# The down projection of a hybrid encoder layer, as eleven tile products or as seven half products of Strassen's scheme

## The reference, cut to what matters

```python
def conv_ffn(h, w_up, conv_w, conv_b, w_down):
    z = h @ w_up                     # 512 x 1024 @ 1024 x 5632
    S = z.shape[1]
    zp = jnp.pad(z, ((0, 0), (CONV_W - 1, 0), (0, 0)))
    zc = conv_b
    for j in range(CONV_W):          # 3 taps along the tokens
        zc = zc + zp[:, j:j + S] * conv_w[j]
    a, u = jnp.split(zc, 2, axis=-1)
    return (jax.nn.silu(a) * u) @ w_down      # 512 x 2816 @ 2816 x 1024
...
    return rms_norm(x, final_norm_g)
```

## Time and profile before

| | |
|---|---|
| median of 3 runs | 965.34 us (965.14 to 965.41) |
| span of the profiled execution | 963.6 us |
| PE, weight loads, DVE, ACT, POOL busy | 99%, 83%, 58%, 41%, 4% |
| share of the chain that ended last | PE 91%, DVE 4%, ACT 3%, issue 1% |
| granted TensorE clock, mean of the core | 0.999 |
| DMA | 93.80 MB, 97 GB/s; 31.4% of the 16 engines |
| matmuls and weight loads | 4782 each |

### The profile page before, as it was taken

How to read it: one execution, slowest core, us unless ns; L and a number is a source line. 1 busy time by engine, 2 the same in 40 slices (tenths; PEclk the granted TensorE clock), 3 DMA queues, 4 the chain that set the end, 5 groups by cost and what they waited for, 6 DMA issues and landing times.

```text
span 963.6 us, 12000 instructions
## 1 busy us (share of the span) xinstructions
PE 951.7 (99%) x4782; PEld 796.8 (83%) x4782; DVE 563.3 (58%) x646; ACT 390.9 (41%) x427; POOL 34.6 (4%) x27
## 2 busy tenths in 40 slices
PE   8999999999999999999999999999999999999997
PEld 6899889777888788888888878888888888888886
DVE  5877654554677564466545548776777677711123
ACT  6473223332664552333333446444434444311122
POOL 1000000200000000000021005000000000000000
PEclk9999999999999999999999999999999999999999
DMA  7414212122232523333223224343333432222212
GB/s 253 160 44 131 73 59 88 46 79 62 66 95 81 178 76 97 98 98 120 90 91 126 79 75 131 88 127 92 87 87 104 113 87 87 92 103 111 88 44 88
DMA packets 121570, 93.80 MB, mean 97 GB/s; under 512 B 3930, under 2 KB 115902, under 8 KB 121406
## 3 DMA queue, kind: packets, MB, share of 16 engines
q1 hardware_dynamic: 121534, 93.27, 31.4%
HBM read 91.16 MB, written 2.10 MB: 97 GB/s over the span
## 4 chain that ended last, share of the span: by engine, by line
PE 91%; DVE 4%; ACT 3%; issue 1%; DMA 0%; SPq 0%; DVEq 0%; ACTq 0%
PE ps L496 66%; PE ps L999 12%; PE ps L860 5%; DVE wL L1345 1%; PE ps L540 1%; PE ps L640 1%; PE ps L631 1%; PE ps L624 1%; ACT wH L1029 1%; PE ps L874 1%; PE ps L890 1%; ACT L1029 1%; PE ps L646 1%; DVE hgF L1345 0%; DVE hgG L1537 0%
## 5 line engine op out<-in xcount | busy, mean ns | idle before, releaser
L496 PE MATMUL ps<-hH,wH 128*128 128x512 f32 x784 | 308.5, 394 | 4.1 <-DVE wL L1345 3.8
L496 PE MATMUL ps<-hH,wL 128*128 128x512 f32 x784 | 305.3, 389 | 0.0
L496 PE MATMUL ps<-hL,wH 128*128 128x512 f32 x784 | 305.2, 389 | 0.0
L1345 DVE TENSOR_TENSOR wL<-raw,wH 128x2048 fp32r<-128x2048 f32 (+3 forms) x90 | 188.4, 2094 | 130.9 <-ACT wH L1029 130.7
L1029 ACT ACTIVATE wH<-raw 128x2048 fp32r<-128x2048 f32 (+3 forms) x90 | 157.7, 1752 | 227.5 <-PE ps L496 146.3
L496 PEld LDWEIGHTS ps<-hH,wH 128*128 128x128 f32 x784 | 147.2, 188 | 37.9 <-DVE wL L1345 5.6
L496 PEld LDWEIGHTS ps<-hH,wL 128*128 128x128 f32 x784 | 147.1, 188 | 31.0
L496 PEld LDWEIGHTS ps<-hL,wH 128*128 128x128 f32 x784 | 147.2, 188 | 30.0 <-issue 0.2
L999 PE MATMUL ps<-wH,actH 128*128 128x512 f32 x176 | 68.7, 390 | 0.0
L999 PE MATMUL ps<-wH,actL 128*128 128x512 f32 x176 | 68.5, 389 | 0.0
L999 PE MATMUL ps<-wL,actH 128*128 128x512 f32 x176 | 68.5, 389 | 0.0
(11 more groups left out here) (275 smaller groups left out, 1225.4 us busy)
## 6 DMA issues: line engine op xcount, KB each, us to landing
raw<-in_w_in SPq DMA_DIRECT2D x57, 512.0 KB, 4.1
raw<-in_w_up SPq DMA_DIRECT2D x44, 512.0 KB, 4.6
raw<-in_w_down SPq DMA_DIRECT2D x22, 512.0 KB, 3.9
raw<-in_w_branch SPq DMA_DIRECT2D x24, 256.0 KB, 4.3
raw<-in_w_out SPq DMA_DIRECT2D x8, 512.0 KB, 4.1
raw<-in_w_mkv SPq DMA_DIRECT2D x8, 512.0 KB, 4.4
xtok<-in_x SPq DMA_DIRECT2D x8, 256.0 KB, 4.4
xtok<-in_x SPq DMA_DIRECT2D x1, 2048.0 KB, 9.1
```

Of the source, the lines that this page charges most:

```text
L496: last = pe.matmul(out_ap, a, b, start=start and k + m == 0, stop=stop and m == 2 and k == len(terms) - 1)
L1345: q.sig(dve.tensor_tensor(out_ap, a, b, op), sem)
```

## The change

**Products.** The down projection A (512 tokens x 2816) by B (2816 x 1024) is cut in halves: tokens, channels 0 to 1407 and 1408 to 2815, columns. By one level of Strassen's scheme (Winograd's form) the eight half products become seven. For each of eleven pairs of channel tiles i and i + 11 there are now two slots: the first with four half products (512 columns of weights, then 1536 of sums), the second, in a later pass over all pairs, with three. A half product is 2 token tiles x 3 matmuls. Slots 77 to 87 are the first pass, 88 to 98 the second; the last two are done together, half product by half product (`for q, b in ((0, 4), (2, 0), (1, 6))`).

**Weight sums** (t1 = b11 + b12, t3 = b12 + b22, t2 = t1 + b22, t4 = t2 + b21) are made in DRAM by transfers that POOL issues: for a pair four copies and four that add to what is there (`accum_op`), 256 KB each, 88 in the kernel, in six steps that wait for one another. Pair i starts when slot 17 + 2i is done (`slot_done` of 18 + 2i), and all of them stand ahead of the `ssqT` additions on POOL.

**Activation sums** are four DVE subtractions or additions of 256 columns for a pair (`act_sums`), after every second up slot. `prod`, `actH` and `actL` are gone: the product goes into `pair`, and its split (`sH`, `sL`, 1024 columns for the first pass, 768 for the second) is made with the slot's weights. The up slots now take tiles i and i + 11 in turn, and the loop of ten turns holds the first twenty of them, with the last two written out behind it.

**End.** The products are combined in PSUM and by DVE (`m1`, `uu`, `uv`, `over`, `added`); x is added as before, by 32 transposes (`residual`). Squares and scaling work on sums in SBUF, POOL multiplies three quarters by the gain in advance, and six stores (before: five) write the result. The load of `gainF` moves on SP from ahead of the up slots to behind the first two loads of the down projection.

```diff
...
         ca = at("ca", B + 4160, [P, S])
         cu = at("cu", B + 4160 + 2 * KIB, [P, S])
-        prod = at("prod", B + 4160 + 4 * KIB, [P, S])
...
+            def load_down(i):
+                n = Slot(N_DN + i)
+                if i < 2:
+                    sp.wait_ge(lo_ready, n.n(-1))
+                else:
+                    sp.wait_ge(d_lo, 3 * (i - 2) + 3)
+                if i == 0:
+                    sp.wait_ge(t_sum, 128 * NP)
+                rows = slice(P * i, P * i + P)
+                sp.dma_start(raw[n.s][:, 0:S], w_down[0, rows, 0:S]).then_inc(raw_in[n.s], 16)
+                sp.dma_start(raw[n.s][:, S:4 * S], t123[rows].rearrange("p q c -> p (q c)")).then_inc(raw_in[n.s], 16)
+            def load_lower(i):
+                s = (N_DN + NP + i) % 2
+                sp.wait_ge(d_lo, 3 * (NP + i - 2) + 3)
+                sp.dma_start(raw[s][:, 0:D], w_down[0, FF // 2 + P * i:FF // 2 + P * i + P, :]).then_inc(d_in[s], 16)
+                sp.dma_start(raw[s][:, D:D + S], t4[P * i:P * i + P, :]).then_inc(d_in[s], 16)
...
-            sp.wait_ge(slot_done, N_MO)
+            with sp.Fori(0, NP) as i:
+                for k in range(2):
+                    load_up(Slot(N_UP + k, i, 2), i + NP * k)
+            for i in range(2):
+                load_down(i)
+            sp.wait_ge(slot_done, N_DN)
             sp.dma_start(gainF[:, :], final_norm_g.partition_broadcast(P)).then_inc(g_row, 16)
-            with sp.Fori(0, KF // 2) as i:
-                for k in range(2):
-                    load_up(Slot(N_UP + k, i, 2), i * 2 + k)
-            for j in range(N_DNS):
...
+            for i in range(NP):
+                rows = slice(P * i, P * i + P)
+                b11, b12 = w_down[0, rows, 0:S], w_down[0, rows, S:D]
+                low = slice(FF // 2 + P * i, FF // 2 + P * i + P)
+                b21, b22 = w_down[0, low, 0:S], w_down[0, low, S:D]
+                t2, t1, t3 = (t123[rows, k, :] for k in range(3))
+                pool.wait_ge(slot_done, N_G0 + 1 + 2 * i)
+                pool.dma_start(t1, b11).then_inc(t_sum, 16)
+                pool.dma_start(t3, b12).then_inc(t_sum, 16)
+                pool.wait_ge(t_sum, 128 * i + 32)
+                pool.dma_start(t1, b12, accum_op=ALU.add).then_inc(t_sum, 16)
+                pool.dma_start(t3, b22, accum_op=ALU.add).then_inc(t_sum, 16)
+                pool.wait_ge(t_sum, 128 * i + 64)
+                pool.dma_start(t2, t1).then_inc(t_sum, 16)
+                pool.wait_ge(t_sum, 128 * i + 80)
+                pool.dma_start(t2, b22, accum_op=ALU.add).then_inc(t_sum, 16)
+                pool.wait_ge(t_sum, 128 * i + 96)
+                pool.dma_start(t4[rows, :], t2).then_inc(t_sum, 16)
+                pool.wait_ge(t_sum, 128 * i + 112)
+                pool.dma_start(t4[rows, :], b21, accum_op=ALU.add).then_inc(t_sum, 16)
             pool.wait_ge(m_T, 4)
             for k in range(2 * KD):
                 pool.wait_ge(x_sq, k + 1)
...
+            def half_product(g, q, b, start, stop, tiles=(0, 1)):
+                s = (N_DN + g) % 2
+                for t in tiles:
+                    ah, al = (x[s][:, q, P * t:P * t + P] for x in (sH, sL))
+                    for m, (x, w) in enumerate(((ah, wH), (ah, wL), (al, wH))):
+                        last = pe.matmul(ps[:, b + t, :], x, w[s][:, S * q:S * q + S], start=start and m == 0,
+                                         stop=stop and m == 2, skip_group_check=True)
+                return last
...
+            for i in range(NP):
+                for q, b in enumerate((4, 6, 2, 0)):
+                    if q == 0:
+                        pe.wait_ge(d_lo, 3 * i + 2)
+                    elif q == 1:
+                        pe.wait_ge(d_lo, 3 * i + 3)
+                    if i == 0 and q >= 2:
+                        pe.wait_ge(taken, N_DN - 3 + q)
+                    last = half_product(i, q, b, i == 0, i == NP - 1)
+                    if i == NP - 1:
+                        last.then_inc(d_sum, 1)
+                if i < NP - 1:
+                    last.then_inc(d_done, 1)
+            for i in range(NP - 2):
+                g = NP + i
+                for q, b in enumerate((4, 6, 0)):
+                    if i == 0:
+                        if q == 0:
+                            pe.wait_ge(d_m1, 1)
+                        else:
+                            pe.wait_ge(d_out, (1, 3)[q - 1])
+                        residual((2, 3) if q == 2 else (0, 1), range(4, 8) if q == 1 else range(4), b)
+                    pe.wait_ge(d_lo, 3 * g + (2, 2, 3)[q])
+                    last = half_product(g, q, b, False, False)
+                last.then_inc(d_done, 1)
+                if i == 0:
+                    pe.wait_ge(d_out, 4)
+                    residual((2, 3), range(4, 8), 2).then_inc(d_sum, 1)
+            for q, b in ((0, 4), (2, 0), (1, 6)):
+                for t in range(2):
+                    for g in (2 * NP - 2, 2 * NP - 1):
+                        pe.wait_ge(d_lo, 3 * g + 3)
+                        last = half_product(g, q, b, False, g == 2 * NP - 1, (t,))
+                    last.then_inc(d_sum, 1)
...
                 tap(1)
-                hi(n + 2)
-                act.wait_ge(f_prod, n.n(1 - N_UP))
-                do(actH[:, bass.ds(n.n(-N_UP), 1), :], prod[:, :], ACT.Copy, f_hi)
+                after()
+            def upper(g, dst, src):
+                do(dst, src, ACT.Copy, d_hi)
+            def down_upper(i):
+                n = Slot(N_DN + i)
+                act.wait_ge(raw_in[n.s], n.loads())
+                if i < 2:
+                    act.wait_ge(slot_done, n.n(-1))
+                else:
+                    act.wait_ge(d_done, i - 1)
+                upper(i, wH[n.s][:, 0:S], raw[n.s][:, 0:S])
+                act.wait_ge(f_sum, 4 * i + 4)
+                upper(i, sH[n.s][:, :, :], pair[:, i, 0:4, :])
+                upper(i, wH[n.s][:, S:4 * S], raw[n.s][:, S:4 * S])
+            def lower_upper(i):
...
+                s = (N_DN + g) % 2
+                if i == 1:
+                    act.wait_ge(d_sum, 4)
+                else:
+                    act.wait_ge(d_done, g - 1 if i == 0 else g - 2)
+                upper(g, sH[s][:, 0:3, :], pair[:, i, 4:7, :])
+                act.wait_ge(d_in[s], 32 * (i // 2 + 1))
+                upper(g, wH[s][:, 0:D], raw[s][:, 0:D])
+                upper(g, wH[s][:, D:D + S], raw[s][:, D:D + S])
             act.wait_ge(n_ms, 2)
             do(rstd_row[:, :], ps[:, 4, :], ACT.Sqrt, n_std, scale=1.0 / D, bias=eps[:, 0:1])
-            ffn(Slot(N_UP))
-            ffn(Slot(N_UP + 1))
-            turns = KF // 2 - 1
...
             with act.Fori(0, turns) as i:
-                q.enter(i, [(hi_ready, 2), (f_tap[0], 2), (f_tap[1], 2), (f_silu, 2), (f_hi, 2)])
+                q.enter(i, [(hi_ready, 2), (f_tap[0], 2), (f_tap[1], 2), (f_silu, 2)])
                 for k in range(2):
-                    ffn(Slot(N_UP + 2 + k, i, 2))
+                    n = Slot(N_UP + k, i, 2)
+                    ffn(n, i + NP * k, lambda: hi(n + 2))
...
+            for k in range(2):
+                ffn(Slot(N_DN - 2 + k), NP - 1 + NP * k, lambda: down_upper(k))
+            for i in range(2, NP):
+                down_upper(i)
...
+            for i in range(NP):
+                lower_upper(i)
+                if i == 0:
+                    act.wait_ge(d_sum, 1)
+                    do(m1[:, :, :], ps[:, 4:6, :], ACT.Copy, d_m1)
+                if i == 4:
+                    act.wait_ge(d_out, 5)
+                    for t in (2, 3):
+                        square_of(t, 1, o_sum)
+                    do(ostat[:, 0, 5:6], eps[:, 0:1], ACT.Sqrt)
+            for t in range(2):
...
+            def ffn(n, i, k, after):
...
-                if lower:
-                    ffn_lower(n + -1)
...
-            def ffn_lower(n):
-                dve.wait_ge(f_hi, n.n(1 - N_UP))
-                j = bass.ds(n.n(-N_UP), 1)
-                tt(actL[:, j, :], prod[:, :], actH[:, j, :].bitcast(F32), ALU.subtract, f_ready)
+                a, u = (t[:, :].rearrange("p (o q t) -> p o q t", o=1, q=2) for t in (ca, cu))
+                dst = pair[:, bass.ds(i, 1), 0:4:3, :] if k == 0 else pair[:, bass.ds(i, 1), 4:7:2, :]
+                tt(dst, a, u, ALU.mult, f_prod)
+                after()
+                if k == 1:
+                    act_sums(i)
+            def act_sums(i):
+                j = bass.ds(i, 1)
+                dve.wait_ge(f_prod, i * 2 + 2)
+                tt(pair[:, j, 2, :], pair[:, j, 6, :], pair[:, j, 3, :], ALU.subtract, f_sum)
+                dve.wait_ge(f_sum, i * 4 + 1)
+                tt(pair[:, j, 1, :], pair[:, j, 0, :], pair[:, j, 2, :], ALU.add, f_sum)
+                tt(pair[:, j, 3, :], pair[:, j, 0, :], pair[:, j, 3, :], ALU.subtract, f_sum)
+                dve.wait_ge(f_sum, i * 4 + 2)
```

(67 more changed lines are left out.)

210 lines of the change are left out of this document (117 added, 93 removed).

## The result

The changed kernel takes **1031.2 us** (median of 4 runs, 1029.7 to 1031.6) beside 965.4 us for the kernel before on the same chip: 1.0676 times as long, 95% interval 1.0661 to 1.0691, 65.9 us more. The forecast was 967.1 us with a range of 956 to 980. Its profiled execution is 64.3 us longer in its span (1027.9 us).

A forecast was written before the change was run, and what follows sets the result against it. The prediction took PE to bound the kernel on average. Its terms, -15.0 + 7.6 + 3.6 + 0.7 + 3.3 + 1.6 = +1.8 us on 965.34, with POOL's transfers at 0, gave 967.1 us, range 956 to 980.

The forecast's parts named there:

- POOL's transfers: Weight sums before the output projection: 2.8 us a step, 17 us a pair, cost 0; PE waits from 20 us a pair.
- rival (c): POOL late, PE stands before the output projection: 980 us at 22 us a pair, 1021 at 26; chance 0.15.
- The matmuls, -15.0: Down projection: 462 matmuls in place of 528, 66 fewer at 0.2268 us each, -15.0 us.
- The up projection, +7.6: Up loop: table load and DVE sums make the chain 22.45 us a turn against PE's 21.77; +7.6 us with late start.
- (a): Up loop: table load not on the chain, or a turn under 21.77 us otherwise; 956.8 us, chance 0.22.
- (e): Up loop: a table load holds the chain longer than its row, two of its 1.28 us; 980 us, chance 0.03.
- Into the down projection, +3.6: Entry of the down projection: chain two slots' work behind, PE waits 3.3 us, then 0.3 for the third piece.
- The second pass, +0.7: Down projection's second-pass slots: conversion and loads hidden; two squares and a root on ACT behind slot 92 cost 0.7 us.
- rival (d): Second pass runs at the pace of its loads, 0.35 us a slot, eleven times; 971 us, chance 0.05.
- The last two slots, +3.3: Slots 97 and 98: slot 98's buffers come free only with slot 96, so PE stands for 3.3 us.
- The tail, +1.6: From PE's last matmul to the span's end: 6.9 us in place of 5.3, +1.6 us.
- Rival (b), the clock: TensorE's clock falls to 1.2 GHz in one of two 3.3 us waits, up to +6.6 us; 970 to 974, chance 0.12.

The follow-up runs named there:

- the first experiment: The changed kernel with the weight sums of pairs 9 to 11 moved behind POOL's additions for the second and third norm: 973.4 us.
- the Silu experiment: The first experiment plus one single-column Silu activation ahead of the up projection's loop, so its table loads go away: 962.4 us.

## Why the prediction was wrong, point by point

**POOL's transfers: the step that failed.** The forecast took 2.8 us a step, the slower of two single rows of transfers between DRAM and SBUF, and from it 17 us a pair and a cost of 0. Measured: 26.9 us a pair in the gate slots, which by the forecast's count of six steps is 4.5 us a step in place of 2.8; in fact five steps hold POOL and the sixth overlaps the next pair's copies, so a waited step took 4.6 to 4.9 us with no other load beside it. The place, the links and the point from which it costs (20 us a pair; 482 us) were right: PE stopped at 485.8 us (forecast 486), and rival (c) at 26 us a pair had the last pair's end at 536 us, measured 535. The mistake was in sizing an unseen operation by the slower of two near rows with bounds of 2.1 and 7.7 us around it, where the threshold, 3.3, lay 0.5 above the value taken. The chance of 0.15 was too small for that. The estimate of 2.6 us a step from the Trainium skill (DMA: Bandwidth & Descriptors, Anatomy of one DMA) was too short as well: the shortest step, one copy alone, took 3.2 us. Its warning that a write to HBM can take long to complete is consistent with that, but no run here separates the write from the read. Which part of a step is issue, read, addition or the reported end stays open.

**The rest of (c)'s price.** Its 1021 us was 10 short: the wait was 1.1 us longer than its 54, the step to the first experiment holds 2.8 us more than the wait, and 6.3 us are those by which the first experiment (973.4) lies above 967.1. Their terms follow.

**The matmuls, -15.0.** 462 of them, as counted. At 0.2333 us in the slots of buffer 1: 6 x 24 + 5 x 18 = 234 by 0.0066 = 1.5 us given back. Not foreseen.

**The up projection, +7.6.** Right in mechanism and nearly in size. The turn was forecast at 22.45 us and is 22.52; the first wait was 2.0, not 1.5 us. So 2.0 + 9 x 0.75 = 8.8 us. Two loads a turn, DVE's `ca` 2.4 us behind `za`'s end (2.3 expected), four sums in 1.65 us (1.65). The run with Silu ahead of the loop shows the cause. That a row decides against the Trainium skill's 2.66 us a switch (ScalarE: Activation LUTs, What ACT_TABLE_LOAD costs) held: by its figure the turn would be 23.8. A tap starts 0.01 us after its load's end here. Rivals (a) and (e) are out.

**Into the down projection, +3.6.** A wait of 2.5 us, behind the first half of slot 77's sums of activations, and 0.5 us of gaps.

**The second pass, +0.7.** A gap of 0.3 us where it was expected, behind the two squares and the root. No slot waited for its load: rival (d) is out, and where the cover was called "barely" it held.

**The last two slots, +3.3.** 3.04 us, at the place named. **The tail, +1.6:** from the last matmul's end to the span's end 7.6 us (6.9 forecast, 5.3 before), +2.3.

**Rival (b), the clock.** It came true in part, and in more places than thought. After the wait of 3.04 us the matmuls came 0.43 us apart, for 1.6 us in all (stretches around it: PE, PEld, DVE, ACT, POOL busy; PEclk):

```profile
1008.00:1011.00 3.00, 0.00 (x0) 0.00 (x0) 2.82 (x5) 1.62 (x3) 0.00 (x0) 1.00 0.00 0
...
1012.00:1013.00 1.00, 1.00 (x4) 0.81 (x3) 0.69 (x1) 0.03 (x1) 0.00 (x0) 0.50 0.00 0
...
1015.00:1016.00 1.00, 1.00 (x6) 0.82 (x5) 0.50 (x1) 0.47 (x1) 0.42 (x1) 1.00 0.00 0
```

The granted clock fell to 1.2 GHz only when PE was back at work and was at 2.4 GHz again within 4 us; in the profiles of the first and the Silu experiment it fell 0.3 and 0.2 us before PE was back. The forecast had up to 6.6 us for this; 1.6 is what it cost. In the change's profile the clock fell behind the waits of 2.0 and 2.5 us too; the first fall cost nothing, for the next two turns would have waited anyway, the second 1.4 us. The Trainium skill (TensorE: Matmul & The Clock Gate, What's actually happening) has an idle stretch throttle the clock, and these rows agree; one profile with the same wait kept its clock (last section).

Put together for the first experiment: -15.0 + 1.5 + 8.8 + 3.0 + 0.3 + 3.0 + 1.6 + 2.3 = +5.5 against +7.8 measured (6.3 to 8.9 by the interval). Two things make up nearly all of the difference. The terms take a wait as PE's idle time; from start to start each of the three longer ones costs 0.3 us more (618.27 to 620.68 for the idle 2.02, and 0.33 to the matmul behind). And in its profile PE is 1.1 us later than before from the first 20 us on, ahead of every edit. The chain shows the same twelve matmuls in the first experiment and before:

```profile
12.79 4.28 PE ps L575 x12
```

```profile
12.93 2.99 PE ps L496 x12
```

Behind waits of 2.14 and 2.10 us the granted clock was 0.50 from 13 to 15 us in the one and 1.00 in the other. From there the profile's parts add up to its whole: +9.2 us to the last matmul of the up projection (845.10; 834.80 before), -4.9 to the last of all (963.48; 958.05), +2.2 behind it, with the 1.1 at the start +7.6 of span.

## What to carry to other kernels

Where a forecast rests on an operation that the trace does not show, and the cost jumps at a threshold between the bounds of its price, the bounds and not the nearest row should set the chance: here it was 58 us for 1.7 us a step more (six steps to a pair). A queue of slow, dependent transfers belongs behind the small operations that others wait for; with three of the eleven pairs moved there, one activation ahead of the loop, the last slots apart and one buffer 64 bytes lower, the same arithmetic runs in 957.5 us, 0.8% under the kernel before. Ahead of a loop, put the table in place that the body ends with, and look in the instruction order whether the body still loads one.
